# A new instruction order on five engines in a chunked RWKV-7 scan, and the guard of its key norms in another form

## What is computed

```
def rwkv_features(h, mu, w_rkv, w0, w1, w2, a0, a1, a2, g1, g2, k_k, k_a, readout):
    ...
    kk = rw_heads(k * k_k).astype(jnp.float32)
    kk = kk / jnp.maximum(jnp.sqrt(jnp.sum(jnp.square(kk), axis=-1, keepdims=True)), 1e-12)
    k_dir = k[None] * (1.0 + (a - 1.0) * k_a)
    ...
def wkv_scan(s0, decay, k, v, kk, a, r):
    def update(s, w_t, k_t, v_t, kk_t, a_t):
        sa = jnp.einsum('ebhvk,ebhk->ebhv', s, kk_t)
        return s * w_t[..., None, :] - sa[..., :, None] * (kk_t * a_t)[..., None, :] + v_t[..., :, None] * k_t[..., None, :]
    ...
    def step(s, inp):
        s = update(s, *inp[:5])
        return s, jnp.einsum('ebhvk,ebhk->ebhv', s, inp[5])
```

## Time and profile before

| what | us |
|---|---|
| median of 3 runs (2529.39 to 2530.75) | 2530.26 |
| time of the profiled execution | 2526.29 |
| span of its trace | 2524.4 |
| start of the running sums of tile 1 to those of tile 7 (six rounds) | 399.45 |
| busy in the span: PE, PEld, DVE, ACT, POOL | 2230.5, 1861.5, 949.1, 685.3, 868.3 |

### The profile page before, as it was taken

The page is one execution under the profiler, slowest core; times in us unless marked ns, Lnnn a source line. Parts: engine busy times, 40 slices in busy tenths (PEclk is TensorE's granted clock), DMA queues, the critical chain, the costliest instruction groups (busy, mean ns, idle before and its releaser), DMA issues. The chain is left out here.

```text
span 2524.4 us, 50949 instructions
## 1 busy us (share of the span) xinstructions
PE 2230.5 (88%) x22528; PEld 1861.5 (74%) x22528; DVE 949.1 (38%) x1500; ACT 685.3 (27%) x1059; POOL 868.3 (34%) x692
## 2 busy tenths in 40 slices
PE   5899989979699999999779996777777787999997
PEld 3787855655499999999639975666666665888786
DVE  3112266970500000122494135666666534000123
ACT  4111175421400000122222134444444223111112
POOL 2223200101143434334043453233333333666662
PEclk8999999989799999999899998899989888999998
DMA  6555520011011121121112442222222212223221
GB/s 257 200 217 197 203 93 17 1 41 52 21 63 64 60 65 60 59 67 59 36 67 90 121 138 54 54 55 51 48 48 52 36 60 87 96 92 99 91 93 66
DMA packets 175510, 210.34 MB, mean 83 GB/s; under 512 B 124792, under 2 KB 133752, under 8 KB 168153
## 3 DMA queue, kind: packets, MB, share of 16 engines
q1 hardware_dynamic: 175320, 207.49, 26.8%
HBM read 184.65 MB, written 22.81 MB: 82 GB/s over the span
## 5 line engine op out<-in xcount | busy, mean ns | idle before, releaser
L254 POOL CAST TMP_r<-WR 128x1024 fp32r<-128x1024 f32 x120 | 126.5, 1054 | 714.7 <-DMA WR<-in_ffn_w_dram 437.5
L273 PE MATMUL PS<-H_r,TMP_r 128*128 128x384 f32 (+1 forms) x1088 | 331.0, 360 | 10.7 <-DVE Y_r L490 10.7
L273 PE MATMUL PS<-Y_r,TMP_r 128*128 128x384 f32 (+1 forms) x1088 | 328.4, 356 | 3.7 <-DVE H_r L490 3.7
L256 POOL TENSOR_TENSOR WR_r<-WR,TMP_r 128x1024 fp32r<-128x1024 f32 x120 | 288.9, 2408 | 9.6
L413 DVE TENSOR_TENSOR P<-TMP,PS 128x768 f32 (+1 forms) x44 | 36.1, 821 | 561.5 <-PE PS L273 561.5
L273 PEld LDWEIGHTS PS<-H_r,TMP_r 128*128 128x128 f32 x1088 | 202.5, 190 | 26.9 <-DVE Y_r L490 11.6
L273 PEld LDWEIGHTS PS<-Y_r,TMP_r 128*128 128x128 f32 x1088 | 201.5, 190 | 19.9 <-DVE H_r L490 4.0
L273 PE MATMUL PS<-H_r,WR_r 128*128 128x384 f32 x736 | 191.6, 342 | 0.0
L396 ACT ACTIVATE TMP<-PS 128x768 f32<-128x768 f32 (+1 forms) x44 | 31.0, 705 | 525.1 <-PE PS L273 525.1
L590 PE MATMUL PS<-H_r,TMP_r 128*128 128x384 f32 x704 | 151.9, 338 | 3.2 <-DVE H_r L628 2.2
L2194 POOL TENSOR_TENSOR scan_small<-scan_small 96x30 f32<-96x30 f32 (+7 forms) x120 | 60.4, 503 | 249.6 <-DMA scan_small<-gram_dram 240.9
(11 more groups left out here) (328 smaller groups left out, 4522.6 us busy)
## 6 DMA issues: line engine op xcount, KB each, us to landing
WR<-in_ffn_w_dram SPq DMA_DIRECT2D x88, 512.0 KB, 3.7
TMP<-in_mod_w_dram SPq DMA_DIRECT2D x40, 1024.0 KB, 5.0
WR<-in_down_dram SPq DMA_DIRECT2D x44, 512.0 KB, 3.5
WR<-in_mix_w_in_dram SPq DMA_DIRECT2D x24, 512.0 KB, 7.0
WR<-in_rw_w_rkv_dram SPq DMA_DIRECT2D x24, 512.0 KB, 4.5
P<-in_mod_w_dram SPq DMA_DIRECT2D x4, 2048.0 KB, 22.1
vkr_dram<-extra SPq DMA_DIRECT2D x16, 384.0 KB, 5.1
scan_front<-vkr_dram SPq DMA_DIRECT2D x16, 384.0 KB, 4.1
```

The source lines that it names most:

```text
L254: nc.gpsimd.tensor_copy(hi, raw).then_inc(weights_hi, 1)
L256: nc.gpsimd.tensor_tensor(lo, raw, hi.bitcast(F32), ALU.subtract).then_inc(weights_split, 1)
L273: last = nc.tensor.matmul(PS[:, bank + b, 0:h1 - h0], w, x[:, h0:h1], start=k + p == 0, stop=k == CT - 1 and p == 2)
```

## The change

The work itself stays the same. What moves:
- The rounds begin one iteration earlier (`range(-3, ...)`) and the pieces of a round stand in another order on all engines, with each wait in front of the piece that needs it.
- ACT: `xx` of tile i comes first in the round. Behind it come `ys` of the tile before, then the Tanhs in turn with the copies of `ta`, `tx`, `tb`. The second pair of Tanhs comes behind the exponentials.
- PE: `l01 l11` move from the end of a round to behind the sweeps `u1`, so that `ta tx tb` follow `mean` at once. `kT_0` and others move within the chain.
- DVE: `yx` moves into the round before, ahead of `cen` and of the running sums. `kd_e`, `accr` and others move too.
- POOL keeps its order (in the first round one MEMSET stands two instructions earlier). SP sends X out first, then Y and the third layout, and puts the loads of G2S behind them.
- The guard `kmax` is `scalar_tensor_tensor` with KROOT as both tensors in place of `tensor_scalar`.

```
@@ rounds @@
-        ROUNDS = [(it, it + 1, it + 2) for it in range(-2, CT + 1)]
+        ROUNDS = [(it, it + 1, it + 2) for it in range(-3, CT + 1)]
@@ marks of ACT, first line @@
-            (0, "xx ta"), (1, "ep_0"), (0, "tx"), (1, "en_0"), (0, "tb"), (1, "first_0 rate_0"), (0, "bv_0"),
+            (0, "xx"), (-1, "ys"), (1, "first_0 t00"), (0, "ta"), (1, "t10"), (0, "tx tb"), (-1, "sq"),
@@ scan_sp @@
-                    for k, src, mark in ((2, YB, "sub"), (0, XB, "turn")):
-                        sp.wait_ge(pool_done, PO[mark, n])
...
+                    sp.wait_ge(pool_done, PO["turn", n])
+                    blocks_out(n, 0, XB, inv16_out)
+                    blocks_out(n, 2, YB, lower_out)
+                    turned_out(n)
                     if here(i):
                         sp.wait_ge(pe_done, PEM["yt", i])
+                    sp.wait_ge(inv16_out, 16 * n + 16)
+                    compact_back(n, 0, XC, x0_in)
+                    sp.wait_ge(lower_out, 32 * n + 32)
+                    compact_back(n, 2, YC, y0_in)
@@ scan_pe @@
                 if here(i):
-                    coupling(i)
+                    pe.wait_ge(act_done, AC["xx", i])
+                    pe.wait_ge(pool_done, PO["off_0", i])
+                    coupled(i, 0, "ta")
+                    pe.wait_ge(pool_done, PO["off_1", i])
+                    crossed(i)
+                    coupled(i, 1, "tb")
+                    pe.wait_ge(dve_done, DV["yx", i])
                     sweep(i, 1, 0)
-                    value_gram(i, 0)
                     sweep(i, 1, 1)
-                    value_gram(i, 1)
+                if here(n):
+                    lora(n, 1)
...
@@ scan_dve @@
-                    DV.done(nc.vector.tensor_scalar(KROOT, KROOT, 1e-12, None, ALU.max), "kmax", c)
+                    DV.done(nc.vector.scalar_tensor_tensor(KROOT, KROOT, 1e-12, KROOT, ALU.max, ALU.max), "kmax", c)
...
+                    mask_last(n, 1)
+                    v.wait_ge(y0_in, 16 * n + 16)
+                    for b in range(4):
+                        last = nc.vector.tensor_scalar(XY[:, 2:4, :, :, BK * b:BK * b + BK].rearrange("p a h j t -> p (a h j) t"),
+                                                       YC, ROWB[:, b:b + 1], None, ALU.mult)
+                    DV.done(last, "yx", n)
```

More of the change, by code:

```diff
@@ L1975, in __init__ @@
                 self.sem, self.made = eng_sem, 0
-                for it in range(-2, CT + 1):
+                for it in range(-3, CT + 1):
                     for ahead, names in order:
@@ L2133, in scan_sp @@
-                if here(n):
-                    if here(i):
-                        sp.wait_ge(pe_done, PEM["cg", i])
+                    sp.wait_ge(dve_done, DV["mA_0", n])
+                    gram_out(n, 0)
+                    sp.wait_ge(dve_done, DV["mA_1", n])
+                    gram_out(n, 1)
+                    blocks_back(n, 0)
+                    blocks_back(n, 1)
+                    if n == 0:
+                        yield
+                        for slot in range(3):
+                            sp.wait_ge(kept_out[slot], 16 * CT)
+                        sp.wait_ge(slots_used, 4 * value.base + 3 * CT)
@@ L2542, in scan_pe @@
                 if here(i):
+                    chain(i, 7)
+                if here(n):
+                    pe.wait_ge(v_in, 16 * n + 16)
+                    tokens(n, "tV", VD[n % 2])
+                if here(i):
                     chain(i, 8)
+                if here(n):
+                    tokens(n, "tK_1", SU[1])
+                if here(i):
+                    chain(i, 9)
                 if here(n):
@@ new lines, in scan_act @@
+                if here(i - 1):
+                    act.wait_ge(dve_done, DV["cen", i - 1])
+                    AC.done(nc.scalar.activation(FIN, YS, ACT.Square), "sq", i - 1)
+                if here(n):
+                    act.wait_ge(dve_done, DV["scan_1", n])
+                    rising(n, 1)
+                    rising(n, 0)
+                    act.wait_ge(pe_done, PEM["l11", n])
+                    tangent(n, 1, 1)
+                    tangent(n, 0, 1)
+                    act.wait_ge(act_done, AC["t01", n])
+                    rate(n, 0)
+                    falling(n, 1)
@@ L2876, in scan_dve @@
-                    DV.done(last, "yx", i)
-                if here(n):
-                    after("kmul", n)
+                    v.wait_ge(pe_done, PEM["u1_0", i])
+                    v.wait_ge(dve_done, DV["yx", i])
+                    sweep(i, 1, 0)
+                    v.wait_ge(pe_done, PEM["u1_1", i])
+                    sweep(i, 1, 1)
+                if here(n):
+                    v.wait_ge(act_done, AC["ep_1", n])
+                    keys(n, 1)
+                if here(i):
+                    v.wait_ge(pe_done, PEM["u2_0", i])
+                    sweep(i, 2, 0)
+                    v.wait_ge(pe_done, PEM["u2_1", i])
+                    sweep(i, 2, 1)
@@ L2943, in scan_dve @@
                     acc = ACC[:, n % 2, :]
[L2944 to L2946 removed]
                     DV.done(nc.vector.tensor_tensor(acc, acc, RDIR, ALU.mult), "accr", n)
                 if here(i):
[L2949 removed]
+                    steps(i, 1)
+                    steps(i, 2)
+                    steps(i, 3)
```

515 lines of the change are left out of this document (253 added, 262 removed), and 33 rows, old and new, of tables (AC, DV, PEM).

## The result

The changed kernel takes 2465.07 us (median of 4 runs, 2462.82 to 2466.45) against 2530.51 us of the kernel before on the same chip: a ratio of 0.9739, 95% interval 0.9719 to 0.9759. That is 65.4 us less; the forecast was 52 us less, 2478 us, with a range of 2461 to 2507. The profiled execution has a span of 2463.0 us, 61.4 less than before.

The account below looks back on a forecast made before the run. A loop of dependencies with list order, no engine, bounds the scan's rounds. Six rounds at 7.0 us (42.0), last first stage 8.1, X's way out 1.0 and guard 1.5 make 52.6 us less: 2478 us, range 2461 to 2507.

Parts of the forecast that it names:

- the first stage: Start of the running sums to end of mA_1 in each round: 26.4 to 19.5 us.
- PE's stops in the sweeps: PE stopping inside the sweeps without waiting for anyone: two stops of 1.03 us a round; more would mean wrong.
- Second to fourth stage: mA_1 to chain 16.6 to 15.9 us; chain 16.1 to 15.3; last step to next sums 7.9 to 8.2.
- The ring of X: Loop from mA_1 through turn, X's transfer, xx, Tanh and gate, and first stage: 59.6 us, setting the round.
- the row at 1792.44: Profile row read as the best time for X's way back, 2.3 us, used in X's 6.9 us out and back.
- The sign of being wrong that came: On DVE: a yx it waits for with the sums behind it was listed as showing the forecast wrong.
- the rest of one `off`: Guard in the chain waits for the rest of one POOL off instruction: 1.3 us, a gain of 1.5 a round.
- The row of `z`: DVE's z in the last tile, 2.71 us beside a POOL TENSOR_TENSOR, taken as waiting for that one instruction's rest.
- Ahead of the sums of tile 1: Stretch before the tile 1 running sums: only the guard shortens, 1.5 us less.
- The end: After the six rounds: last first stage 8.1 us less, X going out first 1.0 less, behind the last ta 0.
- rounds of 58.6 to 61.5 us: The forecast's own case for the length of a round, 2470 to 2489 us in all, chance 0.58.
- all waits go: Rival: PE's stops fall under cover, first stage 17.75 us, ring of X 57.6, total 2463 us; chance 0.17.

Follow-up runs that it names:

- The two moves undone: Changed kernel with yx put back behind the running sums: 2489.75 us; separately, changed kernel with l01 l11 put back ahead of ta: 2483.27 us.
- The run with three steps more: Changed kernel with three of the fifteen steps of POOL's forward substitution done twice in every tile: 2485.07 us, ratio 0.9807 to the kernel before.
- the kernel with the gaps on POOL: Changed kernel with two waits more on POOL, off_0 until turn is done and off_1 until off_0 is: 2460.80 us, ratio 0.9728 to before.

## Why the prediction was right, and where not

- **Where the time lies, and the first stage.** Right. It went from a mean of 25.8 us to 18.8, forecast 19.5 from one round's 26.4; VectorE's work alone came out at 16.9 in the round shown where 17.75 was counted, in part because `kd_0` takes 0.95 us when POOL isn't substituting, and the two sums 1.76 each instead of 3.94 together. The two moves undone confirm that this stage carries the gain. PE's stops in the sweeps are fewer, not more: 7 with 6.1 us in six rounds, against 12 with 12.4; what they go with stands in the last section.
- **Second to fourth stage.** 14.6, 15.8, 7.8 us against 15.9, 15.3, 8.2. The term that was off most is the second stage: the idle time in it was not searched, only one set of products was taken off, and from a single round of 16.6 us where the mean was 15.7.
- **The ring of X, the term that set the sum.** The step that failed: "`mA_1` to end of `turn` ... 27.2 us, which is HBM and POOL and unchanged". Over tiles 2 to 7 it is 24.9 us. The stall by which the prediction priced the guard also works against POOL, and the new order takes five of ten two-input instructions out of POOL's way. X's spreading begins 6.3 to 7.0 us behind `turn` (forecast 6.9), in part by luck: the 2.20 us of the row at 1792.44, taken as the best way back, are SP's issuing of two transfers, and X landed 4.70 us behind its issue there. `xx` to the sums takes 5.9 us (6.0) only where PE waits behind `xx`, in two of six rounds; in the others it takes 7.2 to 7.7, so there this ring isn't the one that binds. From each `mA_1` to the next, from tile 1 to tile 7, the means are 24.6 + 6.6 + 7.0 + 19.0 = 57.2 us, where 27.2 + 6.9 + 6.0 + 19.5 = 59.6 was forecast. The run with three steps more tests it: with a substitution of 18.2 us, near the 17.8 of before, the new order's rounds take 58.8 us. At 1.8 us a round for 3.2 us of substitution, the 2.8 us that went are worth 1.6 of the 2.6 us that the forecast lacked, an estimate from these two runs, whose guards differ too; the rest lies in the other terms. A round gave 9.6 us and not 7.0, and six rounds 57.5 us and not 42.0.
- **The sign of being wrong that came.** "A `yx` that DVE waits for with the sums behind it": VectorE waited for Y for 3.1 and 3.8 us in two of the six rounds. It cost nothing there, since the sums behind it then waited for POOL's gates, which X's ring holds back as well.
- **The guard.** The step that failed: "the rest of one `off`", 1.3 us. It waited through `turn` and both `off`. The row of `z` that the price went by was read rightly, as one instruction's rest, but what it showed didn't carry over to `turn` and the two `off`. The miss cost little: the chain's stage came out at 15.8 us where 15.3 was forecast, and the guard's mean over tiles 2 to 7 is 2.3 us where 1.3 was forecast, and 2.5 before.
- **Ahead of the sums of tile 1.** Forecast 1.5 us less, measured 4.4 more. 3.9 of it lie ahead of the sums of tile 0, where executions differ by up to 5.8 us; the changed kernel's was already 4.4 us behind at VectorE's 601st instruction (1130.5 us against 1126.1), far ahead of anything that was changed. The other 0.5: `kd_0` now stands ahead of `mA_0`, and for tile 0 it met POOL's work on the weights and took 3.12 us, the same lock once more (VectorE, then POOL):

```profile
1496.96 3.12 DVE L2823 TENSOR_TENSOR scan_front<-scan_front 128x768 f32<-128x768 f32 x1
...
1496.31 2.96 POOL L2186 TENSOR_TENSOR WR_r<-WR,TMP_r 128x1024 fp32r<-128x1024 f32 x1
```

- **The end.** Last first stage 9.1 us less (forecast 8.1), `mA_1` of tile 7 to its `ta` 2.1 less (1.0). Behind the last `ta` 2.8 us *more* (0 was forecast): PE is busy for 39.1 us instead of 36.3 with the same 1204 matmuls, at a granted clock of 0.84 where it was 0.88. The clock is not all of it: the kernel with the gaps on POOL, with the same work at 0.91, needs 44.4 us for this stretch, still 1.3 more than the kernel before. The rest is open. The windows of that stretch, columns as above, before, in the changed kernel and in the one with the gaps:

```profile
2004.88:2047.93 43.05, 36.31 (x1204) 30.23 (x1204) 23.64 (x49) 12.66 (x19) 0.00 (x0) 0.88 0.04 7
```
```profile
1940.49:1986.34 45.85, 39.07 (x1205) 31.45 (x1204) 23.13 (x47) 13.07 (x20) 0.00 (x0) 0.84 0.06 15
```
```profile
1927.39:1971.77 44.38, 36.60 (x1205) 29.81 (x1204) 23.13 (x47) 13.06 (x20) 0.00 (x0) 0.91 0.03 6
```
- **The sum.** On the spans 57.5 + 9.1 + 2.1 - 2.8 - 4.4 = 61.5, measured 61.4. The time lay 13 us under the forecast, outside the rounds of 58.6 to 61.5 us that had 0.58 and near the edge of the whole range. The rival "all waits go" had the time nearer (2463) by another road: it needed a first stage of 17.75 us without a stop of PE, and what came was a shorter ring with PE's stops still there. (By its own terms that rival's ring is 57.9 us, not 57.6.)

## What to carry to other kernels

Before a time of one engine is called unchanged, look at what another engine will do beside it in the new order: VectorE's products of two SBUF tiles and GpSimd's instructions exclude each other, and here it was worth 2.8 us of GpSimd's 17.8 in a ring that bound two rounds of six. Instructions of GpSimd that follow each other without a gap can hold up a tiny VectorE instruction for all of them, as `turn` and the two `off` did; a wait that costs 0.08 us between them caps this. And when two waits take turns (the guard's and X's), taking one away gives part of its length.
